# Second block: transposes of the latents and latent query products placed between the steps of a recurrence's chain

## What is computed

```python
def _mixer_block(n, ...):
    p = n @ w_in
    y_a = _rwkv7_time_mix(...)      # recurrence below, then group norm, bonus, gate
    y_b = _mla(q_lat, kv_lat, k_pe, cos, sin, q_norm, w_q_up, kv_norm, w_kv_up)
    merged = sigmoid(gate_a) * (y_a @ w_out_rwkv) + sigmoid(gate_b) * (y_b @ w_out_mla)
    return merged @ w_out

def step(state, inp):               # per token and head, N = 64
    sa = einsum('bhij,bhj->bhi', state, a_t)
    state = state * w_t + sa * b_t + v_t * k_t
    y_t = einsum('bhij,bhj->bhi', state, r_t)

# in _mla
q = (_rmsnorm(q_lat, q_norm) @ w_q_up).reshape(B, S, H, 64 + 32)    # latent query products
kv = (_rmsnorm(kv_lat, kv_norm) @ w_kv_up).reshape(B, S, H, 64 + 64)

# in _rwkv7_time_mix, after the recurrence
y = (y - mean(y)) * rsqrt(var + LNX_EPS) * lnx_w + lnx_b
bonus = sum(r_h * k_h * r_k, -1) * v_h
return (y + bonus) * gate
```

## Time and profile before

| | us |
|---|---|
| three timed runs | 2152.63, 2151.51, 2153.56 |
| their median | 2152.63 |
| span of the profiled execution, from the first to the last instruction | 2150.6 |
| TensorE busy in it | 1896.7 |
| VectorE busy | 915.6 |
| ScalarE busy | 705.2 |
| mean granted TensorE clock | 0.961 |

### The profile page before, as it was taken

The page is one execution under the profiler, slowest core; times in us unless marked ns, Lnnn a source line. Parts: engine busy times, 40 slices in busy tenths (PEclk is TensorE's granted clock), DMA queues, the critical chain, the costliest instruction groups (busy, mean ns, idle before and its releaser), DMA issues.

```text
span 2150.6 us, 37589 instructions
## 1 busy us (share of the span) xinstructions
PE 1896.7 (88%) x16744; PEld 1282.8 (60%) x16744; DVE 915.6 (43%) x1340; ACT 705.2 (33%) x1023; POOL 47.3 (2%) x68
## 2 busy tenths in 40 slices
PE   9999968877768999866766689999999999999998
PEld 7897314332224785312222248677999886779996
DVE  6644201001104754101101137458676574486774
ACT  6644100000003643211111135325544453255443
POOL 2000000000000100000000000000000000000000
PEclk9999989999989999988888899999999999999999
DMA  9266999999999367999999995032853360238540
GB/s 340 98 252 254 420 423 423 425 425 424 428 428 380 120 242 325 427 428 429 428 429 429 429 400 199 4 125 95 265 196 137 123 228 4 92 107 276 185 159 20
DMA packets 142207, 592.53 MB, mean 276 GB/s; under 512 B 5840, under 2 KB 59296, under 8 KB 116720
## 3 DMA queue, kind: packets, MB, share of 16 engines
q1 hardware_dynamic: 140960, 586.68, 68.9%
q0 software_dynamic: 1104, 3.70, 0.5%
HBM read 589.30 MB, written 1.05 MB: 275 GB/s over the span
## 4 chain that ended last, share of the span: by engine, by line
PE 63%; DMA 27%; DVE 4%; ACT 2%; SPq 1%; issue 1%; DVEq 0%; POOL 0%; POOLq 0%; ACTq 0%
PE ps L654 36%; DMA ring<-in_w_up 27%; PE ps L1638 10%; PE ps L3168 3%; PE ps L3217 1%; PE ps L1672 1%; PE ps L1682 1%; PE ps L671 1%; DVE ring_lo L630 1%; PE ps L1567 1%; DMA area<-in_mem 1%; ACT slab_hi L625 1%; PE ps L1211 1%; PE ps L3315 1%; PE ps L3414 0%
## 5 line engine op out<-in xcount | busy, mean ns | idle before, releaser
L1638 PE MATMUL ps<-ring,area 128*32 128x512 f32 x1728 | 275.8, 688 | 154.0 <-DMA ring<-in_w_up 154.0
L630 DVE TENSOR_TENSOR ring_lo<-ring,slab_hi 128x2048 fp32r<-128x2048 f32 (+2 forms) x137 | 302.8, 2213 | 182.4 <-ACT slab_hi L625 182.3
L625 ACT ACTIVATE slab_hi<-ring 128x2048 fp32r<-128x2048 f32 (+2 forms) x137 | 253.3, 1851 | 254.3 <-PE ps L654 237.8
L1638 PEld LDWEIGHTS ps<-ring,area 128*32 128x32 f32 x1728 | 64.8, 124 | 323.5 <-DMA ring<-in_w_up 185.5
L654 PE MATMUL ps<-hT_hi,slab_hi 128*128 128x256 f32 x832 | 234.6, 282 | 0.5 <-DVE ring_lo L630 0.5
L654 PE MATMUL ps<-hT_hi,ring_lo 128*128 128x256 f32 x832 | 233.1, 280 | 0.0
L654 PE MATMUL ps<-hT_lo,slab_hi 128*128 128x256 f32 x832 | 232.9, 280 | 0.0
L2020 ACT ACTIVATE area<-ps 128x512 f32<-128x512 f32 x32 | 19.1, 597 | 548.3 <-PE ps L1638 507.6
L2662 DVE COPY area<-ps 128x256 f32<-128x256 f32 x32 | 13.6, 424 | 411.7 <-PE ps L1543 411.7
L1672 PE MATMUL ps<-ring,area 128*32 128x512 f32 x984 | 122.3, 617 | 55.6 <-DVE area L2693 31.0
L654 PEld LDWEIGHTS ps<-hT_hi,slab_hi 128*128 128x128 f32 x832 | 156.7, 188 | 1.3 <-DVE ring_lo L630 1.1
(11 more groups left out here) (494 smaller groups left out, 3302.7 us busy)
## 6 DMA issues: line engine op xcount, KB each, us to landing
ring<-in_w_down SPq DMA_DIRECT2D x59, 2048.0 KB, 25.5
ring<-in_w_up SPq DMA_DIRECT2D x58, 2048.0 KB, 21.2
ring<-in_w_gate SPq DMA_DIRECT2D x56, 2048.0 KB, 15.7
ring<-in_w_ffn_up SPq DMA_DIRECT2D x44, 1024.0 KB, 8.3
ring<-in_w_in SPq DMA_DIRECT2D x18, 2048.0 KB, 12.8
ring<-in_w_ffn_down SPq DMA_DIRECT2D x10, 2048.0 KB, 8.0
area<-in_w_gate SPq DMA_DIRECT2D x6, 2048.0 KB, 12.9
ring<-in_xattn_w_kv SPq DMA_DIRECT2D x4, 2048.0 KB, 17.1
```

The lines of the kernel that those rows point to most:

```text
L625: return m.nc.scalar.activation(hi, whole, ACT.Copy)
L630: return m.nc.vector.tensor_tensor(lo, whole, hi, ALU.subtract)
L1638: ins = mm(ps[32 * g:32 * g + CAP, 1, :], m.tokT[:, k, :], rows[:, (g % 2) * BANK:(g % 2 + 1) * BANK], start=k == 0, stop=k == KD - 1)
```

## The change

On TensorE the pieces that stood behind the chain now stand between its steps: the six transposes of the latents behind c = 1, the two halves of query product 0 behind c = 3 and c = 4, both halves of product 1 behind c = 5, the first half of product 2 behind c = 6. The second half of product 2 and the whole of product 3 follow behind c = 7, and only then comes `head_sums(0, ...)`. `fill("rest")` moves behind c = 2; it holds no step. The three slots are handed back by the first halves of products 0, 1 and 2 instead of by the transposes. On ScalarE `masks()` moves behind all four copies of query products, and the copies of the transposed latents are written inside `scalar_rwkv`, behind the last gate rows, where they already came. VectorE's program is unchanged.

```diff
@@ tensor_second
     tensor_rwkv(m, pe, l, landed, used)
-    release.extend((W_GATES + PAIRS - 1, W_GATES, W_GATES + 1))
-    tensor_mla(m, pe, l, used, free_released)
+    tensor_mla(m, pe, l, used)
@@ new
+QUERY_STEPS = {3: ((0, 0),), 4: ((0, 1),), 5: ((1, 0), (1, 1)), 6: ((2, 0),), "rest": ((2, 1), (3, 0), (3, 1))}
+
+def turned_latents(m, pe, l):
+
+    pe.wait_ge(*m.at("l_norm", l))
+    for b, tiles in ((2, (0, 1)), (3, (2,))):
+        for i, c in enumerate(tiles):
+            for t in range(NT):
+                ins = m.nc.tensor.transpose(m.ps[:, b, i * T + t * P:i * T + (t + 1) * P], m.lat[:, t, c * P:(c + 1) * P], m.ident)
+        ins.then_inc(m.s("l_T"), 1)
+
+def latent_query(m, pe, l, i, k):
+
+    q_up = lat_slab(m)[2]
+    t, c0, c1 = i // 2, (0, BANK)[i % 2], (BANK, MH * QKD)[i % 2]
+    if k == 0:
+        if i == 0:
+            pe.wait_ge(*m.at("l_cols", l))
+        elif i >= 2:
+            pe.wait_ge(*m.at("q2_rows", l, i - 1))
+    ins = m.nc.tensor.matmul(m.ps[:, 2 + i % 2, 0:c1 - c0], m.latT[:, k, t * P:(t + 1) * P], q_up[:, k, c0:c1], start=k == 0, stop=k == 1)
+    if k == 1:
+        ins.then_inc(m.s("q2_full"), 1)
+    return ins
@@ tensor_rwkv, at the end of each step c of the chain
-    fill("rest")
+        if c == 1:
+            turned_latents(m, pe, l)
+        elif c == 2:
+            fill("rest")
+        for i, k in QUERY_STEPS.get(c, ()):
+            ins = latent_query(m, pe, l, i, k)
+            if k == 0:
+                ins.then_inc(used(W_GATES + (1, 0, PAIRS - 1)[i]), 1)
@@ tensor_mla
-    pe.wait_ge(*at("l_norm", l))
...
+    for i, k in QUERY_STEPS["rest"]:
+        latent_query(m, pe, l, i, k)
     pe.wait_ge(*at("y_cols", l))
     head_sums(0, m.y, "gn_full")
...
+    kv_up = lat_slab(m)[1]
+    for i in range(4):
+        t, out = i // 2, ps[:, 2 + i % 2, :]
+        pe.wait_ge(*(at("q2_rows", l, i + 3) if i < 2 else at("kv2_rows", l, 2 * (i - 1))))
+        c0 = (i % 2) * BANK
+        ins = mm(out, m.latT[:, 2, t * P:(t + 1) * P], kv_up[:, 0, c0:c0 + BANK], start=True, stop=True)
+        ins.then_inc(s("kv2_full"), 1)
@@ scalar_second
     for i in range(4):
         t, c0, c1 = i // 2, (0, BANK)[i % 2], (BANK, MH * QKD)[i % 2]
-        if i == 2:
-            masks()
         act.wait_ge(*at("q2_full", l, i + 1))
         go(m.qm[:, t].rearrange("p h d -> p (h d)")[:, c0:c1], ps[:, 2 + i % 2, 0:c1 - c0], ACT.Copy).then_inc(s("q2_rows"), 1)
+    masks()
@@ scalar_rwkv
     split_first_out()
+    gate_rows("h")
+    for c in range(3):
+        if c != 1:
+            wait("l_T", c // 2 + 1)
+        gain = m.par2("q_g")[:, c:c + 1] if c < 2 else m.par2("kv_g")
+        go(m.latT[:, c, :], half_bank(m, 2 + c // 2, c % 2), ACT.Copy, scale=gain).then_inc(s("l_cols"), 1)
     gate_rows("rest")
```

More of the change, by code:

```diff
@@ L3376, in tensor_rwkv, with tensor_mla @@
                 ins.then_inc(s("y_full"), 1)
-    fill("rest")
-def tensor_mla(m, pe, l, used, free_released):
+        if c == 1:
[6 more added lines that the diff above has]
+                ins.then_inc(used(W_GATES + (1, 0, PAIRS - 1)[i]), 1)
+def tensor_mla(m, pe, l, used):
     nc, ps, at, s = m.nc, m.ps, m.at, m.s
@@ L3633, in scalar_second @@
     scalar_rwkv(m, act, l, lambda: split_out(0))
[L3635 to L3639, removed]
     def masks():
```

## The result

| | median of the timed runs, us | lowest to highest | ratio to before, 95% interval |
|---|---|---|---|
| before | 2152.63 | 2149.98 to 2153.56 | 1 |
| changed | 2163.46 | 2161.43 to 2168.13 | 1.0055 (1.0044 to 1.0066) |

A forecast was written before the change was run, and what follows sets the result against it. The prediction took TensorE, busy 1896.7 of 2150.6 us, as the bound. Late path 7.9 and clock 3.4 added to 2150.6 gave 2161.9 in the span, 2163.9 us by the median; range 2156 to 2168.

The forecast's parts named there:

- The room in the chain: TensorE idles only about 0.1 us per chain step, so moved pieces cost nearly in full; head sums 5.12 us later.
- the last pieces: Query products behind step 7 of the chain, ahead of the head sums on TensorE: 1.72 us.
- the switch from array to chain: TensorE's extra time going from whole-array products back to the chain's 64x64 tiles: 0.07 us.
- The path behind the head sums: Head sums through bonus products and masks to the third key and value product: 8.14 us; 3.97 us late per layer.
- the faster case: Rival: whole kernel becomes faster; with every piece hidden the gain is 1.15 us per layer, 2150.3. Chance 0.03.
- The clock: TensorE's clock falls behind a wait of some 4.6 us at the third product: 1.7 us per layer, 3.4 in all.
- The sum: Whole kernel: 2150.6 + 7.9 + 3.4 = 2161.9 us in the span, 2163.9 by the median.
- The lower end of the range: 2156 us, set over the steady-clock case, also with switches that cost nothing (2160.5 - 2.2).
- The pieces are hidden: Rival: VectorE's updates in the chain hide the query pieces, so no difference, 2151.8 us. Chance 0.08.
- Swallowed behind the stage: Rival: the delay arises but is swallowed later by a load or VectorE running ahead, 2155 to 2157. Chance 0.05.
- The clock stays up: Rival: TensorE's clock isn't lowered behind the wait at the third product, 2160.5 us. Chance 0.26.
- Worse than 2168: Rival: switches at twice their price (+2.2), low clock for longer (+1.6), or late loads. Chance 0.08.

The follow-up runs named there:

- Experiment 3: Changed kernel with VectorE's two bonus products placed around the copies of y, ahead of y_mid: 2150.71 us, ratio 1.0007.
- experiment 8: Kernel before with transposes right ahead of the chain, query product 0 ahead of the head sums, bonus products early, squares right behind the masks: 2153.55 us, ratio 1.0010.
- 12: Changed kernel with bonus products early and query products 0 and 1 together in one gap behind step 3: 2150.25 us, ratio 1.0001.
- experiment 7: Changed kernel with query products 0 and 1 whole in one gap behind step 3, products 2 and 3 behind the chain: 2161.44 us, ratio 1.0046.
- experiments 1: Changed kernel with four unread spare products in TensorE's wait ahead of the third key and value product: 2161.33 us, ratio 1.0055.
- 10: Repeat of the changed kernel with spare products in TensorE's wait: 2161.28 us, ratio 1.0051.
- experiment 5: Changed kernel again, no edit, for a second profile: 2163.27 us, ratio 1.0060 to the kernel before.
- experiment 9: Changed kernel a third time, no edit: 2163.66 us, ratio 1.0059 to the kernel before.
- experiments 4: Changed kernel with the head sums on y ahead of the last three half query products: 2160.29 us, ratio 1.0054.
- 11: Repeat of the changed kernel with head sums ahead of the last query pieces: 2158.61 us, ratio 1.0040.

## Why the prediction was right, step by step

**The room in the chain.** Right. A half put into a step costs 0.86 plus the switches, and the steps grew to 2.10 or 2.11 us, against 1.98 forecast. The head sums came at 13.73 instead of 13.18. By the terms, measured first and forecast behind: step 1 with the transposes 1.86 and 1.83, step 2 1.03 and 1.11, steps 3 to 6 8.43 and 7.92, step 7 0.59 and 0.60, the last pieces 1.82 and 1.72. Nearly the whole error of 0.55 is one mis-sized term, the switch from array to chain. It was taken as 0.07 from a neighbour behind gate products, and behind a query half it is 1436.05 - 1435.00 - 0.86 = 0.19. The switch into the array is 0.15, as forecast. Behind the transposes the way out is 1432.92 - 1432.12 - 0.71 = 0.09, so by these estimates of a piece's own time (0.86 and 0.71) the price depends on what ran before. Why, no run here tells.

**The path behind the head sums.** Right in mechanism and size. The masks start 1449.87 - 1444.79 = 5.08 us behind the head sums (5.18 forecast), the third product 1452.72 - 1444.79 = 7.93 (8.14). With 13.73 the product stands at 21.66 (21.3 forecast, 17.35 before). That is 4.31 later per layer, 3.97 forecast. Experiment 3 shows it by taking the path away: the same late head sums then cost 0.25 at this product.

**One reason in it was wrong.** Against the faster case the prediction said that "`bonus_in` itself would have to come earlier, and it depends on y". It doesn't depend on y. It depends on its place in VectorE's program. Experiment 3 moves it with no other change. The forecast for this kernel wasn't hurt, because the changed kernel leaves it where it was. But the loss is avoidable, which the prediction's wording denies. The conclusion that it wouldn't be faster holds all the same: even with `bonus_in` early (experiments 3, 8 and 12) nothing beats before, since TensorE has only 0.41 us of idle time there to win.

**The clock.** Right that it falls, in both layers of all three executions of the changed kernel that were profiled (and of experiment 7), behind a wait of 4.33 us (about 4.6 forecast). The price was forecast as 1.7 us per layer, within 0 and 2.5. The stages measure it against those of experiments 1 and 10:

| | stage, us | without the fall | price |
|---|---|---|---|
| changed, layers 0 and 1 | 27.56, 28.56 | 25.87 | 1.69, 2.69 |
| experiment 5 | 28.28, 27.31 | 25.87 | 2.41, 1.44 |
| experiment 9 | 27.56, 28.10 | 25.86 | 1.70, 2.24 |

The mean is 2.0. The forecast took only a low stretch of about 3.4 us. In half of the cases it lasts twice as long and starts within the wait. In layer 1 of experiment 5 a short one starts within the wait too, and costs only 1.44. Layer 1 of the changed kernel shows a long one. TensorE's clock in the stretches, where the third product starts at 1894.49:

```profile
1892.00:1893.00 1.00, 0.00 (x0) 0.00 (x0) 1.00 (x4) 1.00 (x4) 0.00 (x0) 1.00 1.03 381
1893.00:1894.00 1.00, 0.00 (x0) 0.00 (x0) 0.93 (x4) 1.00 (x3) 0.00 (x0) 0.57 1.06 391
1894.00:1895.00 1.00, 0.51 (x1) 0.50 (x2) 0.74 (x2) 0.99 (x4) 0.00 (x0) 0.50 1.05 387
...
1899.00:1900.00 1.00, 1.00 (x3) 0.48 (x2) 0.00 (x0) 1.00 (x1) 0.00 (x0) 0.52 0.00 0
1900.00:1901.00 1.00, 1.00 (x6) 0.22 (x9) 0.07 (x1) 0.27 (x1) 0.00 (x0) 1.00 0.00 0
```

It is low from about 1893.1 to 1899.96. Of that, 1899.96 - 1894.49 = 5.5 us is time in which TensorE works, and at half speed half of it is lost, 2.7 us. In layer 0 the fall comes just as the product starts, and half of 3.4 is 1.7.

The prediction named short waits without a fall as the case for a steady clock, and left out that others like them are followed by one. The trace of before has 29 waits of TensorE from 1.17 to 2.37 us. Behind 25 of them the clock stays up. Behind four in the first block (1.51 us twice, 1.66 and 2.37) a stretch at 1.2 GHz starts at their end or at most 0.9 us later. So the length of a wait alone doesn't tell whether the clock falls.

**The sum.** Forecast +7.9 for the path and +3.4 for the clock. The stages show (25.87 - 21.54) x 2 = 8.7 and 4.4, 3.9 and 3.9, in the three executions, together 13.0, 12.5 and 12.6. The timed medians are 10.8, 11.9 and 14.2 us above those of before in their rounds, so the stages account for the loss within the spread of a few us that both kernels show. That the predicted 2163.9 came within 0.5 us of the median is better than the terms are: both were under their traces' values, by 0.8 and about 0.7 us, and the timed loss of that round, 10.8 us, lay below its stages' 13.0. The closeness is luck. The lower end of the range, 2156, has no full sum behind it either: the terms named for it lead to 2160.5 - 2.2 = 2158.3.

**The rivals.** "The pieces are hidden" fell with the steps of 2.10 us. "Swallowed behind the stage" fell too: behind the stages both kernels take 263.2 us in their first profiles, and between them the changed kernel takes 410.58 to 414.21 against 413.09. Nor is there a late load: among TensorE's waits from 1290 us to the end none is for a DMA. "The clock stays up" did not happen in the changed kernel, but in three of four waits of 2.52 us in experiments 4 and 11 it did. "Worse than 2168" got two of its terms in part, switches of 0.34 us a pair instead of 0.22 and the low clock for longer in half of the layers, but the median stayed 4.5 us below.

## What to carry to other kernels

Before work is moved from behind a short dependent chain into its steps, look at TensorE's own rows for the idle time in a step. That another engine looks busy without a gap doesn't mean that TensorE waits. Ask what the moved work had been covering: here the query products hid the path from head sums over bonus products and masks, and without them it turned into a wait of 4.33 us and a fall of the clock, which added half as much again. Before such a wait is accepted as the price, see whether its instructions depend on the late data or only stand behind it in program order, since two instructions moved took nearly all of it away.

## What the runs showed of the hardware that was not expected

One wait of TensorE in an otherwise dense stretch can be enough for 1.2 GHz, and shorter ones have both outcomes. Behind 4.33 us the clock fell in 8 of 8 cases (the changed kernel three times and experiment 7, two layers each). Behind 2.52 us it fell in 1 of 4, with the same program on both sides of the wait. Behind 0.90 us, with spare products ahead of it, it fell in none of 4. The low stretch was about 3.4 or 6.8 us long, and which of them a layer got changed from one execution to the next. The Trainium skill (TensorE: Matmul & The Clock Gate, section "HAM oscillation — how this bites in real kernels") says that waits between bursts of products cost the clock. The traces agree for 4.33 us, with 1.69 and 2.69 us lost per layer in the changed kernel. For waits of 1.5 to 2.5 us they show both outcomes.

Spare products in a wait can shorten a kernel's stage. Eight recorded matmuls more, and the stage went from 27.56 to 25.87 us. In the timed runs this is 2.4 us at most, and not resolved.

Between products in 64x64 tiles and products over the whole array TensorE lost 0.15 us on the way in and, by the estimates above, 0.09 to 0.19 on the way back. The Trainium skill (TensorEngine Tiling (Array Packing), section "Key Properties") says that a change of the tiling mode drains TensorE, and gives no time for it. The rows agree that the change costs time on both sides.

TensorE stands now and then for no other engine: 1.87 us within the chain of layer 1 in experiment 8, and no such wait there in any other profile.
